# Attention stage of a hybrid streaming encoder step: the score units of each pair's second head stand one step later in the order of work

## The chip, the cores and the metric

The kernel runs on one core of one Trainium2 chip. The metric is the device time of one execution in microseconds. TensorE (PE) does the matrix products and the transpositions, PEld is its weight load, VectorE (DVE), ScalarE (ACT) and GpSimd (POOL) do the rest, and SyncE (SP) issues all DMAs.

## The reference

One layer of an encoder step. A prompt of 4096 frames and a sample of 8 x 16 frames pass an RMS norm and one projection that gives two groups of heads. Group A (heads 0 to 7) attends in a window of the own chunk of 64 keys and the two before it, with a learned sink for each head. Group B (heads 8 to 15) attends to the 256 keys that an indexer chooses for each query. Both have a relative bias:

```
s = einsum('bqhgd,bqkhd->bqhgk', q, kg) * HEAD_DIM ** -0.5
s = where(valid, s + bias, -inf);  w = softmax(s)
o = einsum('bqhgk,bqkhd->bqhgd', w, vg)
y = concatenate([oa * silu(ga), ob * silu(gb)]) @ w_out
```

For group B the kernel computes the scores against all keys up to the query's own and adds a mask that is very low where a key was not chosen.

## The kernel before

The program has five stages in a row: projection and choice of keys, attention of the prompt (`stage_two`), output projection of the prompt, choice of keys for the sample, attention and output of the sample. Only the attention of the prompt is touched.

It goes over 32 tiles of 128 queries, and a tile t has six jobs, numbered n = 6t + k. Jobs k = 0 and 1 are four heads of group A each. Jobs k = 2 to 5 are a pair of heads of group B each, with (t+1)*128 keys. A job has steps (`n_steps`, L1119): two for k = 0 and 1, and one for each 512 keys for the others, so 1 in tile 0 and 8 in tile 31.

In a step TensorE transposes up to four blocks of 128 x 128 of the exponentiated scores for each of the two heads (`turn`, L1416, matmuls at L1430). ScalarE copies the first head's transposed bank to pT (L1533), VectorE the second's (L1656). TensorE multiplies the pT of the step before by the values (`apply`, L1433, matmuls at L1459), and so clears the way for the step after. Then come the score units of the job two later, n + 2, that belong to this step (`score`, L1390, matmuls at L1412 for group B and L1403 for group A). The transposes of a step wait for both copies of the step before, since there is one transposition bank for each head. After the last step of jobs 2 and 5 TensorE also transposes the scaled gate (L1468); ScalarE copies it (L1542), and the next job's transposes wait for that copy.

A score unit is one head's keys from c to c + w. `score_units` (L1131) cuts the far keys, all but the last 256, into pieces of 1024 columns, with a narrower piece at the end where they don't divide, and adds the near piece of 256 columns. A job of group B has these pieces for head h = 0 and then for h = 1. Each unit takes the next of two score slots of 1024 columns in PSUM, in the order in which units are issued (`UNIT`). TensorE waits with a unit until VectorE has used the unit two before it. VectorE uses a unit (`use`, L1571, instruction at L1600) by adding mask or bias, writing the sum to the row buffer and keeping the maximum. A wide unit has four matmuls of 512 columns, as q is kept in two parts, and the near unit has two of 256.

There are two row buffers, so job n + 2 writes where job n is read. Therefore `free_at` (L1141) gives each unit the first step of job n after whose transposes its columns are free: in jobs k = 0 and 1 of a tile the second head's half of the buffer is not in use, so that its units stand in step 0 and the first head's in step 1; in jobs k = 2 and 3 both heads' unit of 1024 columns stands in the step that ends it (1, 3, 5), and the last pieces in the last steps. Jobs k = 4 and 5 carry the one unit of jobs 0 and 1 of the next tile.

VectorE's queue follows the same order: in each step the copy of the second head's bank, then the uses of that step's units, at the end of the job the maximum over the pieces (`finish_top`, L1603, instruction L1608). Ahead of the steps of job 1 stands the product of the tile before with its gate (`mix`, L1629, instruction L1636), ahead of job 3 that of group A. Ahead of jobs 2 and 5 stands the scaling of the gate (L1616 to L1625). ScalarE's queue has the copy of the first head's bank and then a share of the exponentials of job n + 1 (L1509).

Of the kernel before, what the change touches and what calls it, by code (L numbers as in the profile page):

```python
# [1108 lines left out]
def a_keys(t):  # L1109

    return P if t == 0 else A_WIDE


def near_of(t):

    return min(NEAR, (t + 1) * P)


def n_steps(n):  # L1119

    t, k = divmod(n, 6)
    return 2 if k < 2 else -(-(t + 1) // 4)
# [8 lines left out]
def score_units(n):  # L1131

    t, k = divmod(n, 6)
    if k < 2:
        return [(0, 0, GROUP * a_keys(t))]
    far = (t + 1) * P - near_of(t)
    cuts = [(c, min(2 * STEP, far - c)) for c in range(0, far, 2 * STEP)] + [(far, near_of(t))]
    return [(h, c, w) for h in range(2) for c, w in cuts]


def free_at(n, unit):  # L1141

    h, c, w = unit
    t, k = divmod(n - 2, 6)
    if k < 2:
        per = 2 * a_keys(t)
        return 0 if h else min(-(-(c + w) // per), 2) - 1
    return -(-min(c + w, (t + 1) * P) // STEP) - 1


N_JOBS = 6 * TILES
UNIT, UNITS_AT = {}, {}
for _n in range(2):
    for _j in range(len(score_units(_n))):
        UNIT[_n, _j] = len(UNIT)
for _n in range(N_JOBS):
    for _g in range(n_steps(_n)):
        UNITS_AT[_n, _g] = []
        if _n + 2 < N_JOBS:
            UNITS_AT[_n, _g] = [_j for _j, _u in enumerate(score_units(_n + 2)) if free_at(_n + 2, _u) == _g]  # L1160
        for _j in UNITS_AT[_n, _g]:
            UNIT[_n + 2, _j] = len(UNIT)
assert len(UNIT) == sum(len(score_units(_n)) for _n in range(N_JOBS))

# [7 lines left out]
_fins = 0  # L1172
for _n in range(N_JOBS):
    for _g in range(n_steps(_n)):
# [7 lines left out]
def exp_pieces(n):  # L1182

    t, k = divmod(n, 6)
    if k < 2:
        return [(0, j * a_keys(t), a_keys(t)) for j in range(GROUP)]
    width = (t + 1) * P
    return [(h, c, min(2 * STEP, width - c)) for c in range(0, width, 2 * STEP) for h in range(2)]


EXPS = {0: 0}
for _n in range(N_JOBS):
    EXPS[_n + 1] = EXPS[_n] + len(exp_pieces(_n))
# [10 lines left out]
def stage_two(nc, rel_bias, sink_a, one_hot, eye, qk_t, gates, values, chosen, ramp, mixed, a_k_prompt, a_v_prompt):  # L1204
    with ExitStack() as ctx:
# [178 lines left out]
        def _(pe):  # L1384
# [88 lines left out]
            before = None  # L1473
            for n in range(N_JOBS):
                for g in range(n_steps(n)):
# [698 lines left out]
```

## Time and profile before

| what | value |
| --- | --- |
| time, median of 3 runs | 5906.38 us (5905.44 to 5907.43) |
| the profiled execution, its own time | 5898.52 us |
| its span | 5896.7 us |
| TensorE matmul busy | 4573.5 us, 78% |
| TensorE weight load busy | 2907.5 us, 49% |
| VectorE busy | 3613.0 us, 61% |
| ScalarE busy | 3291.2 us, 56% |
| GpSimd busy | 1742.4 us, 30% |
| last gate product of the attention stage (L1636) begins | 5004.9 us |

The span is cut into instructions with their start and duration. A row of the timeline merges neighbouring instructions of one engine and kind. Idle time in brackets is the time in which the engine did nothing before the row's first instruction, and the name after it is what ended it. TensorE's granted clock is 1.00 where it ran at 2.4 GHz all the time.

### The profile page before, as it was taken

The numbers are of one execution on the slowest core, as the hardware profiler recorded it, in microseconds if no ns is written. First come the engines' busy times: TensorE is split into PE (matmuls) and PEld (weight loads), VectorE is DVE, ScalarE is ACT, GpSimd is POOL, SyncE is SP. The second block draws the span as 40 slices with busy tenths as digits, with TensorE's granted clock in tenths as the row PEclk, the third lists the DMA queues.
The fourth block names the chain that finished last, engine by engine and source line by source line (L and its number), as shares of the span: only waits on it lengthen the run. The fifth ranks groups of instructions, "written<-read, shape, count | busy, mean of one in ns | idle before, by whom it ended". The sixth has DMA issues, their size and how long they took to land. (4 is left out here: it accounts for less than half of the span.)

```text
span 5896.7 us, 72576 instructions
## 1 busy us (share of the span) xinstructions
PE 4573.5 (78%) x24809; PEld 2907.5 (49%) x24809; DVE 3613.0 (61%) x5854; ACT 3291.2 (56%) x6314; POOL 1742.4 (30%) x1407
## 2 busy tenths in 40 slices
PE   6776787767787667503888888899998998999378
PEld 3443444433343333202666676667776777444145
DVE  1377788888799889893666666665655655001400
ACT  1788788887888779812555555555554554000211
POOL 2355566666585775601221111011010010000000
PEclk9888898888888889755999999999999999999678
DMA  4111011000111100106211111110101000333140
GB/s 128 53 45 39 34 39 35 34 34 27 43 36 37 42 29 34 37 9 125 75 54 49 37 41 36 38 39 26 36 24 36 30 23 17 139 116 103 30 116 4
DMA packets 214791, 284.34 MB, mean 48 GB/s; under 512 B 53232, under 2 KB 143056, under 8 KB 214416
## 3 DMA queue, kind: packets, MB, share of 16 engines
q1 hardware_dynamic: 214432, 279.70, 15.6%
q8 instruction: 207, 3.39, 0.2%
q14 instruction: 152, 1.25, 0.1%
HBM read 168.59 MB, written 112.10 MB: 48 GB/s over the span
## 5 line engine op out<-in xcount | busy, mean ns | idle before, releaser
L1011 DVE TENSOR_SCALAR_CACHE_REDUCE ties<-score,cand 128x512 int8<-128x512 f32 (+14 forms) x480 | 1253.8, 2612 | 141.6 <-POOL score L887 125.2
L570 PE MATMUL bank<-w,x 128*128 128x512 f32 (+1 forms) x2848 | 1241.5, 592 | 24.5 <-DVE w L909 12.7
L779 ACT ACTIVATE act_junk<-score,a_cand,a_sign 128x384 int8<-128x384 f32 (+14 forms) x450 | 990.2, 2201 | 15.0
L1533 ACT ACTIVATE pT<-bank 128x512 f32<-128x512 f32 (+2 forms) x704 | 370.9, 527 | 903.7 <-PE bank L1430 790.9
L570 PEld LDWEIGHTS bank<-w,x 128*128 128x128 f32 x2848 | 570.4, 204 | 603.6 <-issue 534.2
L1509 ACT ACTIVATE row<-row,top 128x1024 f32<-128x1024 f32 (+7 forms) x896 | 759.8, 850 | 88.7 <-DVE top L1590 74.2
L1430 PE MATMUL bank<-ident,row 128*128 128x128 f32 x4728 | 680.9, 280 | 163.7 <-DVE pT L1656 76.1
L1600 DVE CUSTOM_DVE_ANT_0 row<-bank,mask 128x1024 f32<-128x1024 f32 (+7 forms) x576 | 567.7, 1017 | 332.2 <-PE bank L1412 330.8
L1412 PE MATMUL bank<-kT,q_part 128*128 128x512 f32 (+3 forms) x2560 | 639.4, 380 | 115.1 <-DVE part L1600 114.6
L586 PE MATMUL bank<-kiT,qi 128*128 128x512 f32 (+3 forms) x1136 | 395.5, 491 | 423.4 <-ACT relu L709 221.2
L1368 POOL CAST q_part<-q_raw 128x1024 fp32r<-128x1024 f32 x32 | 37.3, 1167 | 2114.4 <-PE bank L1412 1862.9
L1430 PEld LDWEIGHTS bank<-ident,row 128*128 128x128 f32 x4728 | 523.8, 141 | 280.0 <-DVE pT L1656 97.1
L1656 DVE COPY pT<-bank 128x512 f32<-128x512 f32 (+2 forms) x704 | 424.5, 603 | 339.9 <-PE bank L1430 338.4
L1459 PE MATMUL bank<-pT,v 128*64 128x128 f32 x8448 | 592.8, 281 | 0.0
L883 POOL TENSOR_TENSOR score<-score,relu 128x512 f32<-128x512 f32 (+3 forms) x426 | 572.6, 1344 | 33.4
L1412 PEld LDWEIGHTS bank<-kT,q_part 128*128 128x128 f32 x2560 | 430.3, 190 | 291.3 <-DVE part L1600 188.9
L586 PEld LDWEIGHTS bank<-kiT,qi 128*128 128x128 f32 x1136 | 238.5, 233 | 555.6 <-ACT relu L709 290.5
L880 POOL TENSOR_TENSOR relu<-relu,weight 128x512 f32<-128x512 f32 (+3 forms) x426 | 505.4, 1186 | 0.0
L1459 PEld LDWEIGHTS bank<-pT,v 128*64 128x64 f32 x8448 | 452.2, 137 | 97.4 <-issue 96.6
L1716 PE MATMUL bank_out<-wo,mix_in 128*128 128x512 f32 x1024 | 441.4, 594 | 19.9 <-DMA wo<-in_w_out 19.9
L709 ACT ACTIVATE relu<-bank 128x512 f32<-128x512 f32 (+3 forms) x568 | 295.9, 559 | 263.2 <-POOL score L883 176.9
L878 POOL TENSOR_TENSOR score<-relu,weight 128x512 f32<-128x512 f32 (+3 forms) x142 | 154.6, 1089 | 763.9 <-issue 553.5
(220 smaller groups left out, 4781.9 us busy)
## 6 DMA issues: line engine op xcount, KB each, us to landing
qk_t<-ring SPq DMA_DIRECT2D x66, 256.0 KB, 2.0
gates<-ring SPq DMA_DIRECT2D x66, 256.0 KB, 2.0
gate<-gates SPq DMA_DIRECT2D x33, 512.0 KB, 3.5
x<-in_x_prompt SPq DMA_DIRECT2D x32, 512.0 KB, 3.6
q_raw<-qk_t SPq DMA_DIRECT2D x64, 256.0 KB, 4.1
mixed<-mixT SPq DMA_DIRECT2D x64, 256.0 KB, 2.0
mix_in<-mixed SPq DMA_DIRECT2D x32, 512.0 KB, 4.3
x_in<-in_x_prompt SPq DMA_DIRECT2D x32, 512.0 KB, 3.8
```

The costliest lines, as they stand in the source:

```text
L570: ins = pe.matmul(p_bank[n % 2][:, 0:n1 - n0], held[:, c * P:(c + 1) * P], w[:, c, n0:n1], start=(c == 0), stop=(c == KC - 1))
L586: ins = pe.matmul(s_bank[at % 4][:, 0:n], qi[:, part, h * P:(h + 1) * P], kiT[:, c:c + n], start=(part == 0), stop=(part == 1))
L779: tick(act.activation(junk, row, ACT.Sign, bias=c, scale=back, accum_out=a_sum[:, :]))
L880: k = tick(pool.tensor_tensor(r, r, weighs, ALU.mult))
L883: pool.tensor_tensor(to, to, r, ALU.add).then_inc(s_pa, 1)
L1011: n = tick(dve.tensor_scalar(ties[:, 0:width], row, c.bitcast(F32), 0.0, ALU.is_ge, ALU.add, accum_out=counts[:, i:i + 1]))
L1412: ins = pe.matmul(s[:, c0:c0 + m], q_part[:, i, head, :], kT[:, head // GROUP, c + c0:c + c0 + m], start=(i == 0), stop=(i == 1))
L1430: ins = pe.transpose(t_bank[h][:, b * P:(b + 1) * P], held, ident[:, :])
L1459: ins = pe.matmul(oT[0 if k < 2 else 1][h * HD:(h + 1) * HD, col:col + P], value, pT[h][at % 2][:, b * P:(b + 1) * P], start=first, stop=last)
L1509: act.activation(at, at, ACT.Exp, bias=bias, accum_out=out).then_inc(s_exp, 1)
L1600: dve.tensor_tensor_reduce(row[n % 2][:, h, c:c + w], s[:, 0:w], more, 1.0, PAD, ALU.add, ALU.max, part[:, n % 2, h, i:i + 1]).then_inc(s_ ...
L1716: ins = pe.matmul(bank[:, (at % 8) * STEP:(at % 8 + 1) * STEP], m[t % 3][:, c * P:(c + 1) * P], w[:, c, i * STEP:(i + 1) * STEP], start=(c ...
```

## The change

A new function sets the step of a unit. For the jobs of group B (n % 6 of 2 or more) it adds the unit's head, 0 or 1, to the step of `free_at`, but goes no further than the last step of job n - 2. The order in which TensorE issues units and VectorE uses them, and with it the slot of each, comes from this table. The units, their matmuls, the copies, exponentials and DMAs are the same in number and size.

```
+def placed_at(n, unit):
+
+    at = free_at(n, unit)
+    return min(at + unit[0], n_steps(n - 2) - 1) if n % 6 >= 2 else at
...
-            UNITS_AT[_n, _g] = [_j for _j, _u in enumerate(score_units(_n + 2)) if free_at(_n + 2, _u) == _g]
+            UNITS_AT[_n, _g] = [_j for _j, _u in enumerate(score_units(_n + 2)) if placed_at(_n + 2, _u) == _g]
```

In jobs 0 and 1 this leaves step 0 without units and gives step 1 those of both heads, the first head's first. In jobs 2 and 3 the second head's unit of 1024 columns stands in step 2, 4 or 6, or in the last step where there is no later one. Within a step the first head's units still stand ahead of the second's.

## Rows read from the trace of the kernel before

**Rows 1.** Waits of the attention stage, 2757 to 5005 us: total, times, longest.
```profile
PE bank L1412 <- DVE part L1600: 114.6, 177, 1.3
...
PE bank L1430 <- DVE pT L1656: 76.1, 74, 3.1
```

**Rows 2.** Busy time (and instructions) by stretch; then granted clock, DMA share, GB/s.
```profile
2800.00:2900.00 100.00, 83.87 (x629) 64.13 (x627) 65.24 (x190) 51.74 (x162) 22.30 (x9) 0.90 0.24 69
...
4400.00:4600.00 200.00, 178.46 (x1577) 138.96 (x1578) 119.22 (x249) 104.44 (x228) 14.91 (x6) 1.00 0.10 31
```

**Rows 3.** Groups by shape in the attention stage: VectorE's uses of score units.
```profile
L1600 DVE CUSTOM_DVE_ANT_0 row<-bank,mask 128x1024 f32<-128x1024 f32 x360 | 428.9, 1222 | 256.4 <-PE bank L1412 256.3
...
L1600 DVE CUSTOM_DVE_ANT_0 row<-bank,near_bias 128x256 f32<-128x256 f32 x248 | 102.4, 422 | 38.1 <-PE bank L1412 35.7
```

**Rows 4.** Timeline (start, duration), tile 30, job 0, from step 0 to 1.
```profile
4778.73 0.82 DVE L1600 CUSTOM_DVE_ANT_0 row<-bank,mask 128x640 f32<-128x640 f32 x1
4778.86 0.50 PE L1412 MATMUL bank<-kT,q_part 128*128 128x256 f32 x2 [0.61 <-DVE part L1600]
4779.21 0.60 PE L1430 MATMUL bank<-ident,row 128*128 128x128 f32 x4
...
4779.55 0.42 DVE L1600 CUSTOM_DVE_ANT_0 row<-bank,near_bias 128x256 f32<-128x256 f32 x1
...
4780.32 2.11 PE L1412 MATMUL bank<-kT,q_part 128*128 128x512 f32 x8
4781.69 1.23 DVE L1600 CUSTOM_DVE_ANT_0 row<-bank,mask 128x1024 f32<-128x1024 f32 x1 [1.38 <-PE bank L1412]
```

**Rows 5.** Timeline, tile 30: from job 0 to 1; a later pair, job 2.
```profile
4785.99 0.60 PE L1430 MATMUL bank<-ident,row 128*128 128x128 f32 x4
4786.33 0.42 DVE L1600 CUSTOM_DVE_ANT_0 row<-bank,near_bias 128x256 f32<-128x256 f32 x1
...
4786.80 0.16 DVE L1608 TENSOR_REDUCE top<-part 128x2 f32<-128x10 f32 x1
...
4787.51 0.41 DVE L1656 COPY pT<-bank 128x256 f32<-128x256 f32 x1
...
4801.53 0.68 DVE L1656 COPY pT<-bank 128x512 f32<-128x512 f32 x1
...
4802.27 0.66 PE L1430 MATMUL bank<-ident,row 128*128 128x128 f32 x4 [0.49 <-DVE pT L1656]
```

**Rows 6.** Timeline, tile 9, start of job 1.
```profile
3059.16 0.60 PE L1430 MATMUL bank<-ident,row 128*128 128x128 f32 x4
3059.26 1.22 DVE L1600 CUSTOM_DVE_ANT_0 row<-bank,mask 128x1024 f32<-128x1024 f32 x1 [0.74 <-PE bank L1412]
...
3060.55 1.42 PE L1412 MATMUL bank<-kT,q_part 128*128 128x512 f32 x6 [0.20 <-DVE part L1600]
```

**Rows 7.** Timeline of TensorE, tile 29, job 3: steps 1 to 3, and step 6.
```profile
4714.66 2.14 PE L1412 MATMUL bank<-kT,q_part 128*128 128x512 f32 x8
...
4716.64 1.03 PE L1430 MATMUL bank<-ident,row 128*128 128x128 f32 x8
...
4718.63 1.12 PE L1430 MATMUL bank<-ident,row 128*128 128x128 f32 x8
...
4720.69 2.11 PE L1412 MATMUL bank<-kT,q_part 128*128 128x512 f32 x8
...
4730.65 1.21 PE L1412 MATMUL bank<-kT,q_part 128*128 128x512 f32 x4
...
4731.70 0.60 PE L1430 MATMUL bank<-ident,row 128*128 128x128 f32 x4
```

**Rows 8.** Timeline, tile 26, job 2, last step.
```profile
4378.30 0.72 PE L1412 MATMUL bank<-kT,q_part 128*128 128x128 f32 x4
4378.91 0.29 DVE L1600 CUSTOM_DVE_ANT_0 row<-bank,mask 128x128 f32<-128x128 f32 x1
...
4379.27 0.92 PE L1412 MATMUL bank<-kT,q_part 128*128 128x128 f32 x4 [0.25 <-DVE part L1600]
```

## The prediction

> **What bounds the kernel now.** The change touches only the attention stage, about 2757 to 5005 us of the 5896.7 us span; what runs before and after it is the same program. I read first who waits inside that stage [rows 1]: TensorE waits 114.6 us in 177 places for VectorE to free a score slot and 76.1 us in 74 places for a pT copy of VectorE. Together these are 8% of the stage. Then the busy share by stretch [rows 2]: 178.46 us of 200 on TensorE against 119.22 on VectorE and 104.44 on ScalarE, at a granted clock of 1.00, that is 2.4 GHz. So TensorE sets the time, and the question is how much the new order adds to or takes from its waits, step by step, in the timelines.
>
> I write F for a score unit of 1024 columns, P for the narrower far unit where there is one, N for the near unit of 256. A far length of (t-1)*128 columns gives each head of tile t: P N or F N (tiles 2 to 9), F P N or F F N (10 to 17), F F P N or F F F N (18 to 25), F F F P N (26 to 31). VectorE's pitch is the mean duration less the 0.07 us by which read-out and next start overlap: F 1.15, N 0.35 us, 0.133 us for each 128 columns between [rows 3]; call the last far unit's pitch d.
>
> **Jobs 0 and 1 of a tile: one double block in place of two blocks.** They have two steps, and today each step carries one head's units. The transposes of a step and the product of the step before with the values (pT.v) take TensorE about 1.11 us (4779.21 to 4780.32) [rows 4], and in them VectorE drains the block before: N's use begins at 4779.55, 0.34 us after TensorE left the block. After the change step 0 has no units and step 1 has both heads', back to back. The number of instructions is unchanged (no DMA moves either); what counts is which cover goes.
>
> (a) The seam between the heads. A unit takes the slot of the unit two before it and starts 0.13 us after that one's use ends (N at 4778.86 after the use that ended at 4778.73) [rows 4]. The second head's first unit takes the slot of the first head's last far unit. In tile 30 that use ends at 4779.55 at the latest (4779.48 by pitch), so the unit could start at 4779.62 while TensorE is free at 4779.21: 0.41 us of wait that lies under 1.11 us of other work now, and is bare afterwards. In tile 9 the same slot comes free at 3060.55, 1.39 us after TensorE's 3059.16 [rows 6]; 1.19 us of it is new, since 0.20 is waited already. In general, with F taking 1.37 us from issue to VectorE's start (4780.32 to 4781.69) [rows 4], the seam is d+0.24 for two units a head, and d-0.34, not below 0, for three and five. For four it is the same up to 512 columns and 0.49, 0.72, 0.91, 1.17 us above, where TensorE delivers P late. Sums: tiles 2 to 9 7.2, tiles 10 to 17 2.9, tiles 18 to 25 3.7, tiles 26 to 31 1.4 us, 15.2 for one job, 30.3 us for both.
>
> (b) Step 1's transposes in job 1. They follow step 0's directly now, and the second head's bank must have been copied by VectorE for step 0. That copy is queued behind the last uses, the maximum and the mix of the tile before. In tile 30, TensorE leaves the units at 4785.99, and the copy runs from 4787.51 to 4787.92 [rows 5], with 0.06 us to the transposes (4802.27 behind the copy that ended at 4802.21) [rows 5]. They start 1.98 us after the block, where TensorE alone would be there at 1.41. With the second head's transposes and pT.v that makes 2.90 us before the units against 2.22 now: 0.68 us, and seam+0.20 us where VectorE drains longer than 0.7 us. By tiles: 9.0+6.0+6.8+4.2, sum 26.0 us. Behind the stopped transposes wait pT.v and all ten units; VectorE has nothing else then, so nobody fills it.
>
> (c) In job 0 VectorE is free (a gate transposition stands ahead), the copy lands in time, and the second pair of transposes and pT.v costs 1.17 against 1.11 us: 30 x 0.06 = 1.8 us.
>
> Jobs 0 and 1 together: 30.3+26.0+1.8 = 58.1 us.
>
> **Jobs 2 and 3: spread units, and a fuller last step.** Here two heads' F stand in every other step, and the second moves into the empty one. Now a pair of steps takes 6.03 us (4714.66 to 4720.69) [rows 7], and TensorE has no wait in it: transposes, pT.v, transposes, pT.v and eight matmuls follow one another. So there is no wait for the spreading to remove. The eight cost 1.98 us (4714.66 to 4716.64), four cost 1.05 us (4730.65 to 4731.70), and transposes behind units last 1.03 us against 1.12: twice 1.05 less 1.98 less 0.09 is +0.03 us a pair. Some 90 pairs are split: 2 us with the narrow ones. This isn't a form the trace has whole, so the bounds are -0.09 us (only the saved weight load) and +0.19 us (the eight's start-up counted in full), -8 to +17 us.
>
> Where F can't move past the last step, it lands there. Tiles 10, 11, 18, 19, 26, 27: the last step becomes P N F P N for P N P N. Today it takes 1.7 us (P at 4378.30, its use at 4378.91, the next P at 4379.27 after the slot came free, N 0.42 us later and 0.34 us long) [rows 8]. With F third, F starts at +0.97, its use ends at +3.49, the last N waits for that slot until +3.63 and ends at +3.97; less the 0.94 us that F took in its old place this is +1.30 us (128 columns) or +1.38 (256). 3 x 1.30 + 3 x 1.38, in two jobs: 16.1 us. Tiles 4, 5, 12, 13, 20, 21, 28, 29: N P N for N N in the last step. The second N waits until 1.17 us, since the first N's use is 0.35 us and starts at 0.68; about +0.49 us, 8 tiles, 2 jobs: 7.8 us. In tiles with the remainders 0, 1, 6, 7 by 8 the last step gains no wait. Jobs 2 and 3: 2+16.1+7.8 = 25.9 us. Jobs 4 and 5 hold the next tile's jobs 0 and 1 and don't change. ScalarE's exponentials need the maximum at the job's end, at the same distance as now.
>
> **Sum.** 58.1+25.9 = +84 us on the profiled execution's 5898.52 us. The median of the runs shown is 7.86 us over that; the difference carries over: 5906.38+84 = 5990 us, its own range 5966 to 6014 (the bounds of the split pairs, and 10 us for the seams).
>
> **A rule on the clock.** In the stretch 2800 to 2900 the granted clock is 0.90, later 1.00, and it is 1.00 in stretches with 1.3 us slot waits and 3.1 us copy waits in them [rows 1, 2]. The new waits are single ones of 0.4 to 1.7 us. The Trainium skill (TensorE: Matmul & The Clock Gate, HAM oscillation) says that idle gaps between bursts of matmuls can send TensorE back to half clock, each burst then starting cold; by it the early tiles, with the largest new waits, would lose more than the sum says. By that rule, the trace disagrees from 3000 us on, and leaves it open before.
>
> **The rivals.**
> Clock rival: tiles 2 to 9 (about 2795 to 3100 us, at the 84 us of TensorE in a hundred of [rows 2] some 255 us of work) fall from about 0.97 to 0.8: 255 x 0.21 = 54 us more, 6044 us. For it: 0.90 in that region [rows 2]. Against: the gaps stay shorter than ones it stands already.
> Seams hidden: the second head's first unit isn't held, because VectorE keeps closer behind; only (b), (c) and the last steps are left: 84-30 = 54, 5960 us. Against it stands the start 0.13 us after a use [rows 4].
> Spreading pays: VectorE enters the last steps without a backlog, the slot waits of 0.4 to 1.0 us in last steps with P N P N (about 17 us over the stage, part of the 114.6) go, and jobs 2 and 3 cost nothing: 84-26-17 = 41, 5947 us. Against: these waits come from the order within the step, which stays.
> Faster: in jobs 0 and 1 VectorE is the pace, and a double block pays its wait for the first F (1.37 us) once. If the slots let the second head follow directly, a job of tile 30 takes 2.28 + 1.37 + 2 x 4.99 (4781.69 to the end of N's use at 4786.68) - 0.69 = 12.9 for twice 6.78 us now (4779.21 to 4785.99) [rows 4, 5]; 0.6 x 44 jobs (tiles 10 to 31) = -26 us, 5880 us with nothing lost elsewhere. It decides at the seam: VectorE's idle time between N and the next F must be under 0.5 us. By rows 4 it is 1.1 us (N's use ends at 4779.90, F's would start at 4779.62+1.37 = 4780.99).
>
> **How the numbers follow.** Forecast 0.70; seams hidden 0.10; spreading pays 0.08; clock 0.06; faster 0.04; gains and losses cancel 0.02. The range 5940 to 6020 holds the first three but for the forecast's edges. A measurement tells this kernel from no change at about 0.2% (12 us): faster 0.04, within 0.02, slower 0.94.
>
> **What would show it.** In the changed kernel TensorE's slot waits in L1412 groups rise from 114.6 by some 50 us, one of them in the middle of each double block, 0.4 us in tile 30 and about 1.4 in tile 9. Its waits for the pT copy rise from 76.1 by about 20 us, with some 30 more of them, one in each job 1, near 0.6 us in tile 30. A job 0 of tile 30 grows from 13.6 to about 14.1, a job 1 from 13.6 to 14.7 us. A pair of steps in job 2 stays at 6.0 us. The last step of job 2 in tile 26 shows a wait of about 1.7 us ahead of its last N. A double block shorter than twice the old one, or a pair of steps under 5.9 us, would make the prediction wrong, and so would a granted clock under 0.9 after 2900 us.

## The result and the profile after

The changed kernel takes 5986.77 us (median of 4 runs, 5980.38 to 5988.40) against 5906.81 us (4 runs): ratio 1.0134, 95% interval 1.0116 to 1.0151. The forecast was 5990 us. The profiled execution took 5986.31 us with a span of 5984.5 us, 87.8 us over that of before. 2.8 us of these lie ahead of the attention stage, in code that is the same. The stage itself took 85.4 us more, from the first transposes of tile 0 to the last product with the values.

The table gives the length of a job from its first transposes to those of the next job, summed over the 32 tiles, in both profiled executions.

| job of a tile | before | after | change | forecast |
| --- | --- | --- | --- | --- |
| 0 | 288.8 | 303.2 | +14.4 | +17.0 |
| 1 | 275.5 | 308.0 | +32.5 | +41.2 |
| 2 | 482.4 | 497.4 | +14.9 | +13.0 |
| 3 | 422.5 | 440.6 | +18.1 | +13.0 |
| 4 | 356.3 | 359.2 | +2.8 | 0 |
| 5 | 432.1 | 434.7 | +2.6 | 0 |

The waits of TensorE in the stage (total, times, longest; its end moved to 5093 us) answer to [rows 1]:

```profile
PE bank L1418 <- DVE part L1606: 148.1, 227, 1.3
...
PE bank L1436 <- DVE pT L1662: 95.9, 110, 3.1
```

The lines are six further down, so L1418 is L1412 of before, L1436 is L1430 and L1606 is L1600. The slot waits grew by 33.5 us (forecast some 50) and 50 places, the copy waits by 19.8 us and 36 places (forecast about 20 and some 30). These rows hold less than the loss, since the ends of matmuls are modelled: the seam of 0.41 us in the next fence is listed as 0.24. The distances between starts tell it in full.

The seam, timeline of tile 30, job 0, answers to [rows 4]:

```profile
4865.06 0.50 PE L1418 MATMUL bank<-kT,q_part 128*128 128x256 f32 x2 [0.61 <-DVE part L1606]
4865.74 0.42 DVE L1606 CUSTOM_DVE_ANT_0 row<-bank,near_bias 128x256 f32<-128x256 f32 x1
4865.81 2.12 PE L1418 MATMUL bank<-kT,q_part 128*128 128x512 f32 x8 [0.24 <-DVE part L1606]
4867.19 1.22 DVE L1606 CUSTOM_DVE_ANT_0 row<-bank,mask 128x1024 f32<-128x1024 f32 x1 [1.01 <-PE bank L1418]
```

The near unit starts at 4865.06. The second head's first unit could follow 0.34 us later, as the transposes did before (4778.86 to 4779.21), and starts at 4865.81: the seam is 0.41 us to within 0.01, the forecast value. VectorE's idle time behind it is 1.01 us; the faster rival needed it under 0.5.

The same place in tile 9, job 0, answers to [rows 6]:

```profile
3078.49 0.42 DVE L1606 CUSTOM_DVE_ANT_0 row<-bank,near_bias 128x256 f32<-128x256 f32 x1
3078.63 1.43 PE L1418 MATMUL bank<-kT,q_part 128*128 128x512 f32 x6 [1.22 <-DVE part L1606]
```

The unit starts 0.14 us after VectorE began the near unit's use at 3078.49, and all of the 1.22 us is bare now (forecast about 1.4). The prediction counts the end of a use by the start of the next; by its own row the wide use ends 0.07 us later, so that TensorE starts some 0.07 us behind it. The seams are counted in one way throughout, so their sum doesn't change by this. The copy in job 1 of tile 30 answers to [rows 5]:

```profile
4871.47 0.60 PE L1436 MATMUL bank<-ident,row 128*128 128x128 f32 x4
...
4872.28 0.17 DVE L1614 TENSOR_REDUCE top<-part 128x2 f32<-128x10 f32 x1
4872.39 0.69 DVE L1642 TENSOR_TENSOR mixT<-bank,gT 128x512 f32<-128x512 f32 x1
...
4873.00 0.41 DVE L1662 COPY pT<-bank 128x256 f32<-128x256 f32 x1
4873.47 0.44 PE L1436 MATMUL bank<-ident,row 128*128 128x128 f32 x2 [0.43 <-DVE pT L1662]
...
4874.42 2.14 PE L1418 MATMUL bank<-kT,q_part 128*128 128x512 f32 x8
```

The second head's transposes start 2.00 us after the block (forecast 1.98), and the units 2.95 us after it (forecast 2.90). The wait is listed as 0.43 us, where the prediction had named one near 0.6. Job 0 of this tile took 14.07 us (4857.40 to 4871.47), job 1 14.69 us (forecast 14.1 and 14.7).

Steps of job 3 in tile 29, where units were spread, TensorE alone, answer to [rows 7]:

```profile
4799.18 1.21 PE L1418 MATMUL bank<-kT,q_part 128*128 128x512 f32 x4
...
4802.22 1.20 PE L1418 MATMUL bank<-kT,q_part 128*128 128x512 f32 x4
...
4805.24 1.20 PE L1418 MATMUL bank<-kT,q_part 128*128 128x512 f32 x4
```

A pair of steps takes 6.06 us, to 6.03 before. The last step of job 2 in tile 26 answers to [rows 8]:

```profile
4450.71 0.72 PE L1418 MATMUL bank<-kT,q_part 128*128 128x128 f32 x4
...
4451.68 1.36 PE L1418 MATMUL bank<-kT,q_part 128*128 128x512 f32 x6 [0.25 <-DVE part L1606]
...
4454.34 0.51 PE L1418 MATMUL bank<-kT,q_part 128*128 128x256 f32 x2 [1.29 <-DVE part L1606]
4454.68 0.60 PE L1474 MATMUL bank<-ident,scaled 128*128 128x128 f32 x4
```

It lasts 3.97 us from the first unit to the gate's transposes, the forecast length to the digit, with F as the third unit and the last N waiting for its slot. The wait is 1.29 us, not 1.7, since P's two small matmuls of the second head stand in it.

The granted clock (first figure behind the busy times) answers to [rows 2]:

```profile
2800.00:2900.00 100.00, 83.69 (x612) 64.25 (x608) 62.52 (x185) 49.22 (x155) 22.29 (x9) 0.87 0.24 69
...
3200.00:3300.00 100.00, 85.72 (x733) 66.77 (x732) 58.23 (x138) 50.11 (x118) 14.92 (x6) 0.97 0.11 34
4100.00:4200.00 100.00, 89.70 (x794) 70.33 (x794) 57.57 (x114) 51.00 (x107) 7.45 (x3) 0.98 0.10 31
4500.00:4600.00 100.00, 87.58 (x726) 67.56 (x724) 58.63 (x120) 47.86 (x102) 7.45 (x3) 0.98 0.09 27
```

The kernel before has 1.00 in the last three stretches.

### The profile page after: what moved, and what is told of

It is laid out like the page before. It is cut to its first block and busy times, and to the rows that moved or that the text cites. A ratio compares the mean times of both kernels' runs of the same rounds, so it can differ in the third digit from the quotient of the medians.

```text
span 5984.5 us, 72576 instructions
## 1 busy us (share of the span) xinstructions
PE 4607.8 (77%) x24809; PEld 2912.8 (49%) x24809; DVE 3622.0 (61%) x5854; ACT 3287.8 (55%) x6314; POOL 1741.8 (29%) x1407
## 5 line engine op out<-in xcount | busy, mean ns | idle before, releaser
L1436 PE MATMUL bank<-ident,row 128*128 128x128 f32 x4728 | 688.1, 281 | 184.3 <-DVE pT L1662 95.9
L1606 DVE CUSTOM_DVE_ANT_0 row<-bank,mask 128x1024 f32<-128x1024 f32 (+7 forms) x576 | 575.7, 1017 | 411.5 <-PE bank L1418 410.7
L1418 PE MATMUL bank<-kT,q_part 128*128 128x512 f32 (+3 forms) x2560 | 661.2, 385 | 149.2 <-DVE part L1606 148.1
L1436 PEld LDWEIGHTS bank<-ident,row 128*128 128x128 f32 x4728 | 529.9, 142 | 311.6 <-DVE pT L1662 125.0
L1418 PEld LDWEIGHTS bank<-kT,q_part 128*128 128x128 f32 x2560 | 423.3, 190 | 338.3 <-DVE part L1606 235.5
```

What stands on the lines that cost most here:

```text
L1418: ins = pe.matmul(s[:, c0:c0 + m], q_part[:, i, head, :], kT[:, head // GROUP, c + c0:c + c0 + m], start=(i == 0), stop=(i == 1))
L1436: ins = pe.transpose(t_bank[h][:, b * P:(b + 1) * P], held, ident[:, :])
L1606: dve.tensor_tensor_reduce(row[n % 2][:, h, c:c + w], s[:, 0:w], more, 1.0, PAD, ALU.add, ALU.max, part[:, n % 2, h, i:i + 1]).then_inc(s_ ...
```

## The experiments

All times are medians, each with its ratio to the kernel before on the same chip. That kernel took 5903.05 us beside the first four, 5905.74 beside the next four and 5904.69 beside the last two.

**1. Only jobs 0 and 1.**

```
-    return min(at + unit[0], n_steps(n - 2) - 1) if n % 6 >= 2 else at
+    return min(at + unit[0], n_steps(n - 2) - 1) if n % 6 in (2, 3) else at
```

> Only the half of the change in jobs 0 and 1 of a tile (both heads' units in step 1). My theory (the seam between the heads and the wait for the pT copy in job 1): these two jobs cost in the changed kernel 14.4 and 32.5 us more than before, so +47 us against the kernel before, 5954 us, and jobs 2 and 3 stay at 482 and 423 us in sum. Rival (the clock: most of the loss comes because new waits let TensorE's clock fall): well below the share of the rows, +30 us or less, with the low stretches inside the attention stage back to the 34 us of before.

5956.39 us, ratio 1.0091 (1.0077 to 1.0105). Jobs 0 and 1 took 13.7 and 33.6 us more than before, as in the whole change. Jobs 2 and 3 took 1.7 and 1.6 us more. Job 3 of tile 3 took 1.57 and job 2 of tile 27 0.78 us more, and both have low clock in them that they don't have before. Job 2 of the tiles 1 to 3 took 0.98 us more: there the second head's units moved from step 0 to step 1 of job 1, so VectorE comes later to what job 2 needs. In tile 1 the gate's transposes wait 0.34 us for its scaling, where they had no wait before. So 53 of the 80 us belong to this half. The clock isn't its main cause: behind tile 0 the stage spends 48 us at the low level here and 34 in the kernel before (summed from the clock records of both traces), and 14 us at half speed can cost at most 7.

**2. Only jobs 2 and 3.**

```
-    return min(at + unit[0], n_steps(n - 2) - 1) if n % 6 >= 2 else at
+    return min(at + unit[0], n_steps(n - 2) - 1) if n % 6 >= 4 else at
```

> Only the half in jobs 2 and 3 (the second head's unit one step later, at most in the last step). My theory (fuller last steps): by the changed kernel's own job times 15 + 18 us in jobs 2 and 3 and up to 5 in jobs 4 and 5, of which 26 us are waits in the last step: +26 to +38 us, 5938 us in the middle. Rival (spreading pays, the loss all in jobs 0 and 1): within 5 us of 5907 or below.

5940.82 us, ratio 1.0065 (1.0051 to 1.0078), +38 us, at the upper end. The two halves add up to 0.0156, a little over the whole's 0.0134, within the intervals. The clock can account for that: behind tile 0 the stage spends 65 us at the low level in the profiled execution of this half, against 34 before and 55 with the whole change. The 31 us more can cost up to 15 of the 38 us. Job 3 of tile 10, for example, took 2.86 us more than before, 1.53 more than with the whole change, where that job has no low clock.

**3. Spread units, last steps left alone.**

```
-    return min(at + unit[0], n_steps(n - 2) - 1) if n % 6 >= 2 else at
+    return at + unit[0] if n % 6 >= 4 and at + 1 < n_steps(n - 2) - 1 else at
```

> As the half in jobs 2 and 3, but a unit moves only where the step after it isn't the last one, so that last steps keep their units. My theory: a pair of steps stays at 6.0 us, the whole is +2 us against before, within -4 and +8: 5909 us. Rival (spreading pays): the 17 us of slot waits in last steps with four units go, 5890 us. Rival (each smaller group of matmuls costs a start-up): 0.19 us a pair, +17 us, 5924 us.

5906.06 us, ratio 1.0007 (0.9999 to 1.0016). Jobs 2 and 3 grew by 2.0 and 1.8 us for 72 units moved. But 3.1 of these 3.9 us lie in the tiles 12, 13, 20, 21, 28 and 29, where one moved unit joins two narrower ones in a step (0.19 to 0.33 us a job). The other 60 moves cost 0.01 us each (forecast 0.03). TensorE's slot waits are what they were:

```profile
PE bank L1418 <- DVE part L1606: 114.6, 177, 1.3
```

Both rivals fall: spreading takes no wait away, and a smaller group of matmuls pays no start-up of 0.19 us. What jobs 2 and 3 lose, they lose nearly all in their last steps.

**4. The copy ahead of the product with the gate, in job 1** (on the changed kernel, VectorE's queue).

```
-                if k == 1 and t >= 1:
-                    mix(t - 1, 1)
...
                     dve.tensor_copy(pT[1][at % 2][:, 0:cols], t_bank[1][:, 0:cols]).then_inc(s_c1, 1)
+                    if k == 1 and g == 0 and t >= 1:
+                        mix(t - 1, 1)
```

> The changed kernel, but in job 1 VectorE copies the second head's bank ahead of the product with the gate (0.69 us), not behind it. My theory: the transposes of step 1 wait 0.4 to 0.6 us less in tiles 2 to 31, so -14 to -18 us against the changed kernel's 5987, 5971 us. Rival (VectorE is the pace of the double block, the wait for the copy hides nothing that counts): 5987 us, since VectorE's work is the same.

5970.55 us, ratio 1.0115 (1.0101 to 1.0129): -11 us by the ratios. The interval overlaps that of the whole change, so the rows decide. Job 1 took 0.60 to 0.66 us less in each of the tiles 6 to 31 but for two, 14.5 us less in all. It still took 17.9 us more than in the kernel before, not far from the 15.0 that job 0, which hasn't this term, took more in the same run. Timeline of tile 30, job 1:

```profile
4857.04 0.60 PE L1436 MATMUL bank<-ident,row 128*128 128x128 f32 x4
...
4857.92 0.42 DVE L1660 COPY pT<-bank 128x256 f32<-128x256 f32 x1
4858.15 0.69 PE L1436 MATMUL bank<-ident,row 128*128 128x128 f32 x4
```

The copy starts 0.88 us after the block in place of 1.53, and the transposes have no wait. VectorE has the same work, so the rival falls.

**5. The product with the values between the heads** (on the changed kernel, step 1 of jobs 0 and 1).

```
+                    late = n % 6 < 2 and g == 1 and n >= 12
-                    if before is not None:
+                    if before is not None and not late:
                         apply(*before)
-                    before = (n, g)
                     for j in UNITS_AT[n, g]:
+                        if late and j == UNITS_AT[n, g][len(UNITS_AT[n, g]) // 2]:
+                            apply(*before)
                         score(n + 2, j)
+                    before = (n, g)
```

> The changed kernel, but in step 1 of jobs 0 and 1 (tile 2 on) TensorE does the product of step 0 with the values (0.59 us) between the first head's and the second head's units, not ahead of both. My theory (at the seam TensorE waits for a slot): the product covers up to 0.6 us of each seam; min(seam, 0.6) sums to about 9 us over the tiles for one job, so -18 us against the changed kernel's 5987, 5969 us; in tiles 10, 11, 18, 19, 26, 27, where the seam has no wait, nothing. Rival (VectorE is the pace in the double block): its uses end no sooner, 5987 us.

5957.61 us, ratio 1.0090 (1.0074 to 1.0105), outside the interval of the whole change: -26 us by the ratios. Tile by tile the gain of job 0 follows the seam: 0.01 us in tile 10, 0.10 in 11, 0.24 in 12, 0.37 in 13, 0.50 in 14, 0.62 in 15 and 0.76 to 0.79 in 16 and 17 (seams by the prediction 0, 0, 0.14, 0.28, 0.41, 0.55, 0.68, 0.81). Jobs 0 and 1 together took 26.3 us less. In most tiles the gain is some 0.1 us more than the seam; where that comes from no run shows. Timeline of tile 30, job 0:

```profile
4838.56 0.50 PE L1418 MATMUL bank<-kT,q_part 128*128 128x256 f32 x2 [0.61 <-DVE part L1609]
4838.99 0.66 PE L1465 MATMUL bank<-pT,va 128*64 128x128 f32 x8
...
4839.58 2.12 PE L1418 MATMUL bank<-kT,q_part 128*128 128x512 f32 x8
```

The product fills the place of the wait, and the second head's unit needs none. This shows the seam as an uncovered slot wait.

**6. Narrow units first, on the changed kernel; 7. the same on the kernel before; 8. as 7 with the edit of 4.**

```
+        UNITS_AT[_n, _g].sort(key=lambda _j: score_units(_n + 2)[_j][2])
         for _j in UNITS_AT[_n, _g]:
             UNIT[_n + 2, _j] = len(UNIT)
```

> The changed kernel with the units of a step issued in the order of their width, narrow ones first. My theory (slot waits come from a unit that stands two behind a wide one with only a narrow one between): a double block of tile 30 falls from 11.8 to about 10.6 us, one of tile 10 from 6.0 to 3.8, a last step with P N F P N by 0.9 us; VectorE's backlog at the block's end grows by 0.9 us and lengthens the waits for the copy in jobs 1 and 2 by about as much, together -50 us against the changed kernel: 5937 us. Rival (the order within a step only moves the waits): 5987 us.

> The kernel before with the units of a step issued in the order of their width, narrow ones first. My theory: a block of jobs 0 and 1 loses 0.8 to 0.9 us of slot waits from tile 10 on (88 blocks, -70 us), last steps with four units lose 0.4 us (-6 us), and the copy wait in job 2 grows by 0.9 us (+20 us): -56 us, 5851 us. Rival (the waits only move): 5907 us.

> The same order, with the copy ahead of the product with the gate in job 1. My theory: in the kernel before the transposes of step 1 in job 1 follow a block of units, so the copy is in time by more than 2 us and the product's place counts little: 0 to -5 us against the sorted kernel before, 5849 us. Rival (VectorE's backlog of the wide last unit makes the copy late there as well): -10 us or more.

On the changed kernel 5962.24 us, ratio 1.0098 (1.0084 to 1.0112). On the kernel before 5864.64 us, ratio 0.9931 (0.9919 to 0.9943), and with the edit of 4 5865.18 us, 0.9930. So the order within a step is worth 41 us without the change and only some 20 with it, to 56 and 50 forecast. In the kernel before job 0 of tile 30 fell by 1.59 us, as expected for its two blocks. But its job 1 fell by 0.76 us only, and job 2 grew by 12.1 us in all tiles. VectorE ends a block with a wide unit now, and what stands behind it comes later. In tile 30 of experiment 7, start of job 2:

```profile
4769.30 1.03 PE L1431 MATMUL bank<-ident,row 128*128 128x128 f32 x8
4769.63 1.22 DVE L1601 CUSTOM_DVE_ANT_0 row<-bank,mask 128x1024 f32<-128x1024 f32 x1
...
4771.44 0.69 DVE L1626 TENSOR_TENSOR scaled<-gate,rinv 128x512 f32<-128x512 f32 x1
4772.05 0.68 DVE L1657 COPY pT<-bank 128x512 f32<-128x512 f32 x1
4772.79 0.44 PE L1431 MATMUL bank<-ident,row 128*128 128x128 f32 x2 [1.29 <-DVE pT L1657]
```

The wait was 0.49 us [rows 5]. The edit of 4 gives nothing there, as expected: in job 1 a block of units stands between the copy and the transposes that need it.

**9. The copy ahead of the scaling of the gate, on the kernel before; 10. the same with narrow units first.**

```
-                if k == 2:
-                    scale_gate(t, 0)
...
-                if k == 5:
-                    scale_gate(t, 1)
...
                     dve.tensor_copy(pT[1][at % 2][:, 0:cols], t_bank[1][:, 0:cols]).then_inc(s_c1, 1)
+                    if g == 0 and k in (2, 5):
+                        scale_gate(t, 0 if k == 2 else 1)
```

> The kernel before, but in jobs 2 and 5 VectorE copies the second head's bank of step 0 ahead of the scaling of the gate (total, reciprocal, product: 1.06 us), not behind it. My theory (what stands ahead of that copy is waited for in full, as in job 1 of the changed kernel): the 0.5 to 1.4 us wait in job 2 goes in tiles 6 to 31, about -17 us, and in job 5 that of tiles 4 to 11 shrinks, up to -10 us; in job 5 from tile 12 on the wait of 1.1 us stands in job 4 as well and comes from group A's unit, so it stays. -20 to -27 us, 5882 us. Rival (the gate's transposition becomes late instead): within 5 us of 5906.

> The kernel before with narrow units first within a step and the copy ahead of the scaling of the gate. My theory: narrow units first gave -41 us although the wait in job 2 grew by 12 us; with the scaling behind the copy 1.06 us of it go in each tile, so -41 - 30 - up to 10: 5830 us, the fastest of all. Rival (the two gains share the same wait): no faster than the better of the two alone, 5865 us.

5874.23 us, ratio 0.9950 (0.9937 to 0.9962), 30 us under the kernel before (forecast 20 to 27), and 5826.68 us, ratio 0.9867 (0.9852 to 0.9882), the fastest of all, 78 us under it. In 9, job 2 took 20.3 us less and job 5 5.6. Job 2 of tile 30 in experiment 10:

```profile
4736.86 0.69 DVE L1653 COPY pT<-bank 128x512 f32<-128x512 f32 x1
4737.47 0.16 DVE L1617 TENSOR_TENSOR total<-a_sums,lsink 128x8 f32<-128x8 f32 x1
4737.61 0.66 PE L1431 MATMUL bank<-ident,row 128*128 128x128 f32 x4 [0.22 <-DVE pT L1653]
```

The wait of 1.29 us is 0.22, and the gate's scaling follows where nothing waits for it. The two gains add up, so the rival of a shared wait falls.

## Why the prediction was right, point by point

**The bound.** TensorE sets the stage's time: each cover taken from it showed in full, and the copy moved by 0.65 us in experiment 4 moved the job by as much.

**(a) The seam.** Right in mechanism, and in size from tile 9 on but for tile 31. Job 0 of the tiles 10 to 22 grew by the seam and 0.06 us within 0.15 us in each tile (0.32 for 0.34 in tile 13, 0.87 in tile 17, -0.03 in tile 10). In tile 31 it grew by 0.23 us for 0.61: the block of the kernel before has 0.36 us more slot wait there than its other block. Experiment 5 shows the cause.

**(b) The copy in job 1.** Right: from tile 12 on job 1 grew by 0.82, 0.96, 1.09, 1.30, 1.56, 1.82 us by the sum and by 0.85, 0.96, 1.11, 1.28, 1.55, 1.85 us in the trace. Experiment 4 shows that what stood ahead of the copy was waited for. In tiles 10 and 11 it was 0.96 and 0.71 for 0.68. In the tiles 6 to 9, where the sum had 2.2 to 2.8 us, it was 0.1 to 0.4 us less.

**Where (a) and (b) failed: tiles 2 to 5.** The sum took for them 5.3 us of seams and 3.5 of copy waits, but jobs 0 and 1 took 3.6 us less than before. The step that failed is the table of steps. I took it that the first head's units all stand in step 1 before the change, but `free_at` compares with 512 columns, and in tiles 2 to 5 the far unit, in 2 and 3 the near one too, is free in step 0. So four units stood in step 0 of the tiles 2 and 3 and three in step 0 of the tiles 4 and 5, and the change moves the second head's into step 1: there it spreads units where the prediction has it gather them. Start of tile 3 in the kernel before, both heads' units in step 0:

```profile
2827.92 1.22 PE L1412 MATMUL bank<-kT,q_part 128*128 128x256 f32 x4
2829.38 1.22 PE L1412 MATMUL bank<-kT,q_part 128*128 128x256 f32 x4 [0.24 <-DVE part L1600]
```

And in the changed kernel, where each step has one head's units:

```profile
2830.18 1.22 PE L1418 MATMUL bank<-kT,q_part 128*128 128x256 f32 x4
...
2832.84 0.74 PE L1418 MATMUL bank<-kT,q_part 128*128 128x256 f32 x4
```

No timeline of [rows 4 to 8] lies in these tiles. Not all of the 3.6 us is the order's: these jobs have 14.7 us of low clock in them to 18.6 before, worth up to 2 us. In tiles 6 to 8 the opposite was missed: job 0 has a copy wait of its own as well (0.56 us in tile 6), because VectorE still uses group A's unit there. Jobs 0 and 1 together came out at +46.9 us for 58.1, the largest miss. No run varies the small tiles by themselves, so this account rests on the table of steps and these rows.

**Jobs 2 and 3.** The spread pairs cost 0.01 us each in experiment 3 for 0.03. Its steps with a moved unit and two narrower ones don't occur in the whole change, which moves the second of these on. P N F P N cost 1.32 and 1.33 us in tile 10, 1.37 in job 2 of tile 18, 1.40 and 1.38 in tile 26 (forecast 1.30), 1.43 and 1.41 in tile 19, 1.46 twice in 27 (1.38). N P N cost 0.44 to 0.65 us in the tiles 12, 13, 20, 21, 28 and 29 (0.49). In tiles 4 and 5 it cost 0.59 and 0.46 us in job 3, but 0.94 and 0.89 in job 2. The term came out at +33.0 us for 25.9. Some 6 us of the excess stand in four jobs with low clock (below), 1.0 us in job 2 of the tiles 1 to 3 (experiment 1).

**A term that was missing: job 4.** In the tiles 8, 9, 16, 17, 24 and 25 job 4 grew by 0.46 to 0.54 us, 3.0 us in all. There job 3's last step ends with N F N or N P N where it had N N. So VectorE enters job 4 later, and its copy for the first step stands behind those uses and the maximum. The transposes of the second step wait for it. Tile 17 before and after:

```profile
3590.22 0.69 DVE L1656 COPY pT<-bank 128x512 f32<-128x512 f32 x1
...
3590.70 1.10 PE L1430 MATMUL bank<-ident,row 128*128 128x128 f32 x8
```

```profile
3637.64 0.69 DVE L1662 COPY pT<-bank 128x512 f32<-128x512 f32 x1
...
3638.38 0.66 PE L1436 MATMUL bank<-ident,row 128*128 128x128 f32 x4 [0.32 <-DVE pT L1662]
```

The prediction had put this at nothing, with the sentence that jobs 4 and 5 don't change.

**The clock.** It moved, but not where the rival put it. In the stretch 2760 to 3050 us the granted clock is 0.93 before and 0.92 after. Later on, where it was 1.00 throughout, single stretches fell to 0.97 and 0.98 (fence above). One of them begins at the end of job 2 of tile 11. The timeline of TensorE, and the granted clock by stretch (1.00 and 0.50, behind the busy times):

```profile
3210.91 0.54 PE L1418 MATMUL bank<-kT,q_part 128*128 128x256 f32 x2 [1.23 <-DVE part L1606]
...
3212.98 1.97 PE L1436 MATMUL bank<-ident,row 128*128 128x128 f32 x8 [0.69 <-ACT gT L1548]
...
3214.88 1.98 PE L1465 MATMUL bank<-pT,v 128*64 128x128 f32 x16
```

```profile
3210.00:3211.00 1.00, 0.09 (x1) 0.09 (x1) 1.00 (x3) 0.00 (x0) 0.00 (x0) 1.00 0.00 0
3211.30:3212.00 0.70, 0.70 (x5) 0.59 (x3) 0.38 (x2) 0.00 (x0) 0.00 (x0) 0.50 0.00 0
```

Elsewhere such groups take 1.03 to 1.12 us. That is the low level, 1.2 GHz. Ahead of the fall TensorE had waited 0.43 and 1.23 us for slots in the last step of job 2. The 0.69 us for the gate's copy come behind the fall, and stand in the kernel before as well. Job 3 of this tile grew by 3.78 us, of which 2.4 are gone in experiment 4, where the order is the same but the clock stayed high. With the end of job 2 of tile 11 (0.5 us), job 3 of the tiles 3 and 18, job 0 of the tiles 23 and 27 and job 5 of the tiles 4 and 7 (0.7 to 1.6 us each) this makes some 10 us. The clock records bear that size out: behind tile 0 the stage spends 34 us at the low level before and 55 after, and 21 us at half speed cost at most 10, about a tenth of the loss. The Trainium skill (TensorE: Matmul & The Clock Gate, HAM oscillation) has it that idle gaps between bursts of matmuls can send TensorE to half clock; there the gaps are long waits for DMAs. The trace agrees in part: the clock fell in the kernel with more waits, but no wait of TensorE in the jobs concerned from 3050 us on is over 1.3 us, and none of these is for a DMA. Nor do the waits alone tell where or how much: experiment 7 has 54.5 us of slot waits, half those of the kernel before, and yet 51 us at the low level, and the places differ from kernel to kernel. So what makes the clock fall stays open.

**The total.** +84 us forecast, +80 by the medians and +85 inside the stage by the profile. The closeness is partly luck: 12 us too many in tiles 2 to 5 stand against 3 us of job 4, some 10 us of low clock and a little in jobs 2 and 3 that were not in the sum.

## What to carry to other kernels

Ask of each piece of independent work between two uses of a double buffer how much of the other engine's drain it covers; moving units so that such cover stands where nothing waits costs the uncovered part each time, though no instruction is added. With two slots, a wide unit followed by a narrow one makes the third wait for nearly the whole wide use: issue narrow units first, and keep what others wait for (a copy) ahead of what nobody waits for (a scaling, a product) in the queue of the engine that drains. And check the table of an order in the smallest cases too, where a formula with a threshold behaves differently.

## What the runs showed that I had not expected

From 3050 us on the granted clock fell for short times, though TensorE is busy for 86 to 90% in the stretches around them and no single wait in the jobs concerned is over 1.3 us; in the profiled execution of the kernel before it stayed at 1.00. Each such time cost a job 0.7 to 2.4 us. Moving the scaling of the gate behind a copy and sorting the units of a step by width, edits that change no amount of work, gave 1.33% together, as much as the change studied here took.
